# Gathering, turning and scoring all cached K during the projections of a hybrid decoder step

## The reference

```
q, k, v, z, f = split(rms_norm(x) @ w_in_attn)
logf = log_sigmoid(f + b_f);  c = cumsum(logf)
s = q.k / 8 + c[query] - c[key]          causal
y = (softmax(s) @ v * silu(z)) @ w_out
```

## Time and profile before

| | us |
|---|---|
| median of 3 runs (range) | 2210.48 (2210.18 to 2215.91) |
| the profiled execution's own time | 2207.72 |
| span of its trace | 2206.0 |
| projections, 797 to 1200 | 403 |
| seam and batch 0, 1200 to 1321 | 121 |
| batches 1 to 7, 1321 to 2058 | 737 |
| tail, from 2058 | 148 |

### The profile page before, as it was taken

One profiled execution on the slowest core, in us unless ns is written; L12 is line 12 of the kernel. 1 busy time (PEld: TensorE's weight loads), 2 busy tenths in 40 slices (PEclk: granted clock), 3 DMA queues, 4 the chain that ended last, 5 costly groups with the idle time before them and its releaser, 6 DMA issues. The chain is left out here.

```text
span 2206.0 us, 36290 instructions
## 1 busy us (share of the span) xinstructions
PE 1884.8 (85%) x13168; PEld 1343.1 (61%) x13168; DVE 1126.3 (51%) x1846; ACT 538.1 (24%) x1203; POOL 610.2 (28%) x691
## 2 busy tenths in 40 slices
PE   4999999999999799999997568776777786778797
PEld 3877777787787677887886244443444443434475
DVE  4444444454464561112231676766676767676523
ACT  4211211121121332112111123232323232323421
POOL 0000000000000001001001676665666665666010
PEclk9999999999999999999998679898988898989899
DMA  4111111111111213223225779999999999999861
GB/s 139 39 45 48 36 49 48 40 50 43 40 41 48 97 58 102 93 76 97 93 76 138 268 221 342 348 342 330 336 362 329 352 325 330 339 344 337 294 220 59
DMA packets 184781, 384.64 MB, mean 174 GB/s; under 512 B 21009, under 2 KB 99250, under 8 KB 184366
## 3 DMA queue, kind: packets, MB, share of 16 engines
q1 hardware_dynamic: 126796, 196.59, 26.3%
q0 software_dynamic: 57376, 185.06, 25.0%
q10 hardware_dynamic: 466, 0.88, 0.1%
HBM read 353.94 MB, written 29.22 MB: 174 GB/s over the span
## 5 line engine op out<-in xcount | busy, mean ns | idle before, releaser
L332 POOL DMA_INDIRECT k_raw<-in_cache_k_dram,k_idx x512 | 496.3, 969 | 285.4 <-DVE kt L1525 140.9
L1525 DVE STREAM_TRANSPOSE kt<-k_raw 128x1024 f32<-128x1024 f32 x256 | 315.0, 1237 | 108.3 <-DMA k_raw<-in_cache_k_dram,k_idx 106.6
L876 DVE TENSOR_TENSOR w_lo<-w_raw,w_hi 128x1024 fp32r<-128x1024 f32 x96 | 109.0, 1135 | 332.9 <-ACT w_hi L516 330.3
L673 PE MATMUL ps_a<-h_hi,w_hi 128*128 128x512 f32 x656 | 263.6, 402 | 0.0
L675 PE MATMUL ps_a<-h_hi,w_lo 128*128 128x512 f32 x656 | 258.6, 394 | 0.0
L674 PE MATMUL ps_a<-h_lo,w_hi 128*128 128x512 f32 x656 | 258.6, 394 | 0.0
L1273 PE MATMUL b<-con,p_p 128*128 128x128 f32 x432 | 89.2, 322 | 134.8 <-DVE p_p L1539 91.4
L425 POOL DMA_DIRECT2D out_dram<-g_out x4 | 2.2, 543 | 628.7 <-ACT g_out L563 628.7
L1273 PEld LDWEIGHTS b<-con,p_p 128*128 128x128 f32 x432 | 52.3, 155 | 177.7 <-DVE p_p L1539 77.9
L1251 PE MATMUL b<-kt,q_bd 128*32 128x256 f32 x2048 | 139.8, 419 | 19.7 <-DVE q_n L1550 19.5
L673 PE MATMUL ps_b<-h_hi,w_hi 128*128 128x512 f32 x384 | 153.0, 398 | 0.0
(11 more groups left out here) (295 smaller groups left out, 3135.5 us busy)
## 6 DMA issues: line engine op xcount, KB each, us to landing
v_pg<-in_cache_v_dram SPq DMA_DIRECT2D x256, 512.0 KB, 6.4
w_raw<-in_w_in_pool_dram SPq DMA_DIRECT2D x32, 512.0 KB, 4.0
w_raw<-in_w_in_attn_dram SPq DMA_DIRECT2D x32, 512.0 KB, 4.3
w_raw<-in_w_out_pool_dram SPq DMA_DIRECT2D x16, 512.0 KB, 3.6
k_raw<-in_cache_k_dram,k_idx POOLq DMA_INDIRECT x512
d_sb<-decay POOLq DMA_DIRECT2D x32, 256.0 KB, 7.7
qa<-q_aug POOLq DMA_DIRECT2D x8, 528.0 KB
ka<-k_aug POOLq DMA_DIRECT2D x8, 528.0 KB
```

Of the source, the lines that this page charges most:

```text
L332: pool.indirect_dma_start(k_raw[:, k, i, :], None, cache_rows, bass.IndirectOffsetOnAxis(ap=row, axis=0)).then_inc(k_full[k], 16)
L673: nc.tensor.matmul(ps, ah, bh, start=j == 0, stop=False)
L876: V.tensor_tensor(w_lo[slot][:, 0:width], raw[:, 0:width], w_hi[slot][:, 0:width].bitcast(F32), ALU.subtract).then_inc(dve_lo, 1)
L1525: V.transpose(kt[s % 2][:, :, 64 * k:64 * k + 64].rearrange("p i (t c) -> p t i c", c=32), k_raw[:, k, :, :].rearrange("p t (i c) -> p t i ...
```

## The change

All K work leaves the attention block. Whole rows of 4 KB are gathered, 4 indirect DMAs of 128 rows for a unit, so that a unit is now 128 rows of each of the four pages of a group with all 16 heads; there are still 64 units. DVE turns them during the projections, and PE scores one unit after each half of a prompt tile, 32 matmuls of 128 columns. ACT copies the scores out and stores them to `s_scr`; the attention block reads them back beside the decay. For this, q of all samples is made first, from eight raw weight tiles `wq`, and `sample_tile` of n = 0 falls away. silu(z) is stored to `z_scr` and read back when attention begins. The stores of q, k and rows move from POOL to SP, and V's first pages and `w_o` are loaded earlier. In the diff below some stretches are summed up in words; they stand in parentheses or after the name of an engine.

```diff
-    C_KB: 8 index columns;  cache_rows = cache_k[0] as half rows
+    C_KB: 4 index columns;  cache_rows = cache_k[0].rearrange("n k h d -> (n k) (h d)")
+        def k_quad(pool, u):
+            for k in range(4):
+                if u:
+                    pool.wait_ge(dve_kt, 4 * (u - 1) + k + 1)
+                pool.indirect_dma_start(k_raw[:, k, :], None, cache_rows,
+                                        bass.IndirectOffsetOnAxis(ap=k_idx[:, u, k:k + 1], axis=0)).then_inc(k_full[k], 16)
...
 SP, projections
+                sp.wait_ge(...); w_tile(0, 0), then w_query(k) for the eight wq tiles, spill of x1, wf
+                for f in range(KT8):
+                    for n in range(4):
+                        (waits as before) w_tile(f, n)
+                        n == 0: store_k(f - 1)       n == 1: store_k_rows(f - 1)
+                        n == 2: store_v_rows(f - 1)  (with k_sample and z_scr[f - 1])
+                        n == 3: store_q(f)
+                sp.wait_ge(pe_qk, UNITS)
+                for p in range(VR):
+                    v_load(sp, 1, p).then_inc(v_full[p], 16)
 POOL, projections
+                pool.wait_ge(spill, 16)
+                pool.wait_ge(dve_xn, 18)
+                pool.wait_ge(pe_pre, 1)
+                pool.wait_ge(dve_ix, 1)
+                for u in range(UNITS):
+                    (u == 12, 32: gather of the cached logf)
+                    (u == 60: qk_pair(pool, 0), v_pair(pool, 0))
+                    k_quad(pool, u)
 ACT, projections
+                def unit_out(b, s):
+                    u = b * QUADS + s
+                    act.wait_ge(pe_qk, u + 1)
+                    past(act, st_s[s % 2], b * (8 * QUADS) + 16 * (s // 2))
+                    nc.scalar.copy(ss_st[s % 2][:, :, :].rearrange("p h k -> p (h k)"), b5[:, 0:2 * PAGE]).then_inc(act_su, 1)
+                    act.wait_ge(act_su, u + 1)
+                    act.dma_start(s_scr[bass.ds(b, 1), :, :, PAGE * s:PAGE * s + PAGE].rearrange("o p h k -> p (o h) k"),
+                                  ss_st[s % 2][:, :, :]).then_inc(st_s[s % 2], 16)
 PE, projections
+                for half in range(2):            (made once: q of the samples)
+                    for k in range(KT8):
+                        mm = nc.tensor.matmul(ps_b[r:r + TS, c], h_s[:, k, :], wq[k][:, c], ...)
+                def unit_scores(b, s):
+                    past(pe, act_su, b * QUADS + s)
+                    pe.wait_ge(dve_kt, b * (4 * QUADS) + (4 * s + 4))
+                    for hh in range(2):
+                        for j in range(4):
+                            for cg in range(4):
+                                i = 16 * hh + 4 * cg + j
+                                mm = nc.tensor.matmul(b5[32 * cg:32 * cg + 32, PAGE * hh:PAGE * hh + PAGE], q_bd[:, i, :],
+                                                      kt[s % 2][:, i, :], start=j == 0, stop=j == 3, tile_position=(0, 32 * cg))
+                    mm.then_inc(pe_qk, 1)
+                proj:  n > 0: sample_tile
+                       half_tile(0), row_turn(j=0) for n >= 2, unit_scores(f, 2n)
+                       half_tile(1), add_parts for n > 0, row_turn(j=1) for n >= 2, unit_scores(f, 2n+1)
 DVE, projections
+                for n: lo; for j in 0, 1: rows_copy (n >= 2); k_turn(8f + 2n + j + 2); unit_queries(f + 1) at n = 3, j = 0
+                def k_turn(u):
+                    if u >= 2:
+                        dve.wait_ge(pe_qk, u - 1)
+                    for k in range(4):
+                        dve.wait_ge(k_full[k], 16 * (u + 1))
+                        V.transpose(kt[u % 2][:, :, 32 * k:32 * k + 32], ...).then_inc(dve_kt, 1)
...
 attention
-    PE: sample_scores(b, s) in each slot;  DVE: k_turn x4 in each slot, 16 copies into q_bd for a batch
-    POOL: k_quads in each slot
+    POOL: z_t[0], z_t[1..7] once; score_half loads s_in beside d_sb
+    DVE: sample_scores(b, s // 2) at even s: 2 adds of 128x256 from SBUF and one reduce
-    SP: w_o after pe_new of the last batch
+    SP: w_o in batch NB, ahead of its last 24 V pages, into tiles that wait for nothing
```

More of the change, by code:

```diff
@@ new lines, in build @@
+        pt_all = place("pt_all", [P, NB * PAGES], I32, big_at(AT_U + UW))
+        AT_K = 34584
+        k_raw = place("k_raw", [P, 4, DM], F32, big_at(AT_K))
+        kt = [place(f"kt{i}", [P, 32, PAGE], F32, big_at(AT_K + 4096 * (i + 1))) for i in range(2)]
+        wf = w_raw[1][:, :].rearrange("p (k n) -> p k n", n=P)
+        wq_at = [big_at(33792 + 1024 * k) for k in range(4)] + [big_at(AT_Y + 2048), at_in + 1280, big_at(19456), big_at(21504)]
+        wq = [place(f"wq{k}", [P, DM], F32, wq_at[k]) for k in range(KT8)]
@@ L257, in build @@
[L257 to L265, removed]
+        VR = 8
+        SW = PAST // 4 + TS
@@ L270, in build @@
[L270 to L277, removed]
+        wo_at = [big_at(n) for n in (9024, 10048, 0, 1024, 4160, 5184, 6208, 7232)]
@@ L593, in proj @@
                 def proj(f, first, last):
                     for n in range(4):
-                        ahead = first and n == 0
-                        if not ahead:
-                            px(f * 4 + (C_L0 + 2 + n + CR_W))
-                        if not ahead and not (last and n == 3):
+                        if n:
+                            px(f * 3 + smp_at(0, n))
+                        if not (first and n == 0) and not (last and n == 3):
                             act.wait_ge(ld_w[(n + 1) % 2], f * 32 + 16 * (33 + (n + 1) // 2))
@@ new lines, in proj @@
+                        unit_scores(f, 2 * n)
+                        half_tile(1, ps, slot, h_hi, h_lo, KT8).then_inc(tile_done, 1)
+                        if n:
+                            pe.wait_ge(act_px, f * 3 + (1 + PX_L0 + 1 + n))
+                            pe.wait_ge(act_b7, b7_at)
+                            add_parts()
+                        if n >= 2:
+                            row_turn(f, n, 1, more)
+                        unit_scores(f, 2 * n + 1)
+                        if n >= 2:
+                            pe.wait_ge(act_b7, b7_at + 1)
+                            nc.tensor.transpose(b7[0:TS, 0:P], (ks_st, vs_st)[n - 2][:, :], ident).then_inc(pe_b7, 1)
@@ L819, in _ @@
+                proj(0, extra(0))
+                forget_rows()
+                with pe.Fori(1, 3) as f:
+                    proj(f, extra(1))
+                page_totals(0, 2)
+                with pe.Fori(3, 6) as f:
+                    proj(f, extra(3))
+                page_totals(1, 5)
+                with pe.Fori(6, KT8) as f:
+                    proj(f, extra(6))
             @block.vector
@@ new lines, in page_decay @@
+                def page_decay(t):
+                    dve.wait_ge(pe_tri, t + 1)
+                    total = V.tensor_tensor(tot[:, t, :], tot[:, t, :], b4[:, 0:NH], ALU.add)
+                    total.then_inc(dve_tm, 1)
+                    dve.wait_ge(dve_tm, 1 + 12 * (t + 1) + 2 + t)
+                    for h in range(NH):
+                        last = V.tensor_scalar(pfx[:, h, :], pfx[:, h, :], -1.0, tot[:, t, h:h + 1], ALU.mult, ALU.add)
+                    last.then_inc(dve_dec, 1)
@@ L1599, in gate @@
                     r = P * QBLOCKS[s]
+                    first = isinstance(b, int) and b == 0
+                    dve.wait_ge(ld_z[0 if first else 1], 16)
                     z = z_t[:, bass.ds(b, 1), r:r + P].rearrange("p o t -> p (o t)")
@@ L1619, in sample_out, with batch @@
                     V.tensor_reduce(o_n[:, :], o_raw[:, :, :].rearrange("p h d -> p d h"), AX, ALU.add).then_inc(dve_ov, 1)
-                def batch(b, sample, more):
-                    if sample is False:
-                        for k in range(KR):
-                            k_turn(b, 0, k)
+                def batch(b, sample):
                     queries(b)
                     for s in range(SLOTS):
-                        ahead = (b, s + 1) if s < SLOTS - 1 else (b + 1, 0)
-                        ahead = ahead if more or s < SLOTS - 1 else None
                         prompt_max(b, s, 0)
```

637 lines of the change are left out of this document (352 added, 285 removed).

## The result

The change makes the kernel slower: 2249.7 us (median of 4 runs, 2238.4 to 2259.0) against 2213.2 us for the kernel before on the same chip; the ratio is 1.0159 with a 95% interval of 1.0106 to 1.0212. The forecast was 2160 us, faster. The profiled execution of the changed kernel took 2248.77 us with a span of 2247.0, 41 us more than the span before.

A forecast was written before the change was run, and what follows sets the result against it. PE was taken to bound the projections and DMA the attention. The terms 177 - 3 - 50 - 163 - 9 = -48 took the span from 2206 to 2158, forecast as 2160 us, with 2105 to 2230 for 8 in 10.

The forecast's parts named there:

- Projections: Projection stage: grows by 177 us, of which 163 for 64 units at 2.55 us and 12 for late K.
- Seam: Between projections and attention: 10 us becomes 7, since POOL no longer ends with stores; -3.
- Batch 0 with its stall: First attention batch and the wait before it: 112 us becomes 62, since nothing waits for K; -50.
- Batches 1 to 7: Later attention batches: 105.3 us each becomes 82, bounds 63 and 92; -163 over seven.
- Tail: After the batches: w_o loaded earlier ends ACT's wait for it; -9 (0 to -12).
- first rival: Projections: K's supply paces them, 10 us a unit, 2230 us in all, deciding from about 9.7; chance 0.17.
- late K: Projections: waits for K whose buffer slot returns late, 12 us (0 to 60).
- the 81 of the slots: Batches 1 to 7: 105.3 us less 19 from eight slots and 5 from the q/k wait.
- second rival: Batches 1 to 7 stay near 90 us as sample_scores filled PE's waits; 2218 us in all; chance 0.13.
- 10.5 us of other work: Batch start, kernel before: work covering part of ka's 16.3 us load, leaving about 8 us of PE idle.
- The slots' 62 us: Batch 0: 58 us from a line through two worked slots, 62 with new_scores, last values and a late q/k load.
- The upper bound (75): Batch 0: 75 us if the clock stays at the 0.76 seen before the change.

The follow-up runs named there:

- e11_supply: Changed kernel with a quarter of each unit's score matmuls in the projections, gathers and turns as they are: 2236.5 us.
- e4_nogather: Changed kernel with K's gathers left out in the projections, all but the first unit's: 2209.8 us.
- e13_nosupply: Changed kernel with a quarter of each unit's score matmuls and no gathers but the first unit's: 2137.6 us.
- e10_half: Changed kernel with 8 filler matmuls a slot in all batches and no other edit: 2210.4 us.
- c5_fill_half: Changed kernel with two q/k buffer pairs, lsel and half of w_o earlier, V pages behind stores, filler matmuls per slot (16 in batch 0, 8 later): 2163.9 us.
- e2_qk2: Changed kernel with two pairs of q/k buffers, batch b+1's heads loaded from slot 1 of batch b: 2217.4 us.
- e3_ends: Changed kernel with lsel loaded in the projections, first V pages behind the last stores, all of w_o loaded at the attention's start: 2227.4 us.
- e9_kraw2: Changed kernel with two buffers for gathered rows and one for turned ones, which also changed VectorE's order: 2296.1 us.

## Why the forecast was wrong

| Step | Forecast | Measured |
|---|---|---|
| Projections | +177 | +179 |
| Seam | -3 | +9.6 |
| Batch 0 with its stall | -50 | -30 |
| Batches 1 to 7 | -163 | -113 |
| Tail | -9 | -4.4 |
| Sum | -48 | +41 |

**Projections: the sum held, its terms did not.** That +177 met +179 is luck. A unit of 64 records takes 1.96 us on TensorE, not 2.55: splitting 256 columns into 128 cost next to nothing. With the few units that ran at the lower clock all 64 took 132 us, for 163. What filled the gap is waiting: VectorE's 120 us for `k_raw`, TensorE idle for 44 of the 576 us (6.5 of 403 before), and a clock of 0.96 for 1.00. The first rival's mechanism was thus at work. K's supply holds the stage at 575 us even with a quarter of the matmuls (e11_supply), 9.0 us a unit, under the 9.7 from which I let it decide; TensorE's own part is 546 (e4_nogather). Either alone covers most of the other, as e13_nosupply shows. The trace gives its length. On each of the four buffers, on the mean, 7.4 us pass from the start of a gather to the start of its turn (its landing, counted from the same start, has a median of 6.3), the turn takes 1.2, and 0.4 later the next gather starts: 9.0 us, in e11_supply too. The prediction had named this loop, "must come back within a unit's 8.9 us less its turn and issue, about 7 us", but had no row with a landing time and took 12 us for late K. That term was too small, as the 2.55 was too large.

Whether the loop's 6.3 us is a latency or the queues' load is only in part settled. For a latency: the four gathers of e4_nogather, with no other unit's behind them, landed in 5.4 to 7.0 us, median 6.1. Against it: DMA is busy 0.93 of the stage.

The rule of the Trainium skill weighed in the prediction (SBUF — State Buffer, "SBUF: two separate sides") does not show here either: GpSimd's gathers, beside a VectorE busy for 419 of 576 us, lasted as long as before in the median (937 for 946 ns); the mean rose from 969 to 1011 and the longest to 1.66 us. No row tells whether VectorE's turns run in a two-port mode, so the rule itself was not tested. The gathers' line, min/median/max in ns:

```profile
L347 POOL DMA_INDIRECT k_raw<-in_cache_k_dram,k_idx x249: 932/937/1655, 802.0 to 1364.0; - x125
```

**Batches 1 to 7: the step that failed.** "PE pauses more, and some stretches will stay at half clock. I take 82": 1 us was set aside for that, over the 81 of the slots. The slots' savings were read from matmuls of which most ran at the high level; once `sample_scores` was gone, the granted clock fell from 0.89 to 0.84. Give TensorE half of that work back as filler and a batch falls from 88.8 to 85.8 us (e10_half), or beside the second q/k pair from 85.4 to 81.4 (c5_fill_half), although the filler keeps TensorE busy for 9 us of it (56.6 over six batches): what the clock cost is these 3 to 4 us and whatever the filler itself takes. (Of e10_half's 3 us a batch, 1.3 are a shorter wait for `ka`.) This is the second rival, that `sample_scores` was what TensorE did while it waited; I gave it 0.13.

The other part is the q/k load. I had shortened it to 11 us "with K's 2 MB out of the queues"; it takes 15.1 us from issue to landing, nearly as before (16.3), since V's pages are what it shares the queues with. The one load with no V page under way, that for batch 1, shows it:

```profile
1471.13 8.03 DMA ka<-k_aug
```

The prediction's 10.5 us of other work behind the issue was misread too: 16.3 less 10.5 is not the 8 us of idle time that it names. Before, TensorE stood idle for 8.9 us at that place, so 7.4 were covered; in the changed kernel 15.1 less 7.7 is 7.4 again. TensorE's idle time stayed at 7.7 us a batch for the 3 forecast; e2_qk2 shows 4 us a batch for it. The two parts together are the 7 us that the forecast's 82 missed, and with both mended (c5_fill_half) the batch takes 81.4. That this is the forecast's figure is in part chance: the forecast kept 3 us of wait for q and k, and had no filler to run.

**Batch 0.** The slots' 62 us came from slots at full clock. It ran at 0.52, that is nearly all at 1.2 GHz, though TensorE was busy for 69 of 82 us: nothing but short transposes and scores with pauses between them. The upper bound (75) took the clock at 0.76, that of a batch with units in it; this bound was itself an effect of what the change removes. With filler it is 66 us (e10_half) to 75 (c5_fill_half). The step that failed is the same as in the batches: durations at the full clock were kept for a stretch that lost the work between its pauses.

**Seam.** I looked for POOL's stores, which did go, and did not follow SP's queue past the block's end: eight page loads in front of the last stores, then `lsel`. e3_ends shows that, taken together, all but 2.6 us of the 19 were this.

**Tail.** `w_o` waits for no semaphore any more, but SP's queue reaches it only at 2103.37, the end of the last batch: the V pages ahead of it are issued as TensorE frees their buffers. So ACT's first cast waited longer than in the earlier trace rows:

```profile
2113.75 1.04 ACT L1661 CAST wo_hi<-w_o 128x1024 fp32r<-128x1024 f32 x1 [7.78 <-DMA w_o<-in_w_out_attn_dram]
```

Loaded at the attention's start it leaves the chain (e3_ends). Seam and tail failed alike: a wait was taken away, and what stood ahead in SP's queue was not counted.

Left open: how much of the projections' +179 comes back with gathers a unit ahead, be it with room for both pairs of buffers (memory did not allow it) or with e9_kraw2's buffers and `lo` left where it was; and why 8 filler matmuls a slot do better than 16.

## What to carry to other kernels

Work on TensorE that fills its waits costs little there (8 added matmuls a slot made the changed kernel 39 us faster, 16 a slot 3 us slower). Moved to a stage where TensorE has no wait, it can be paid for twice: once in the new stage, which here grew by 179 us through the matmuls and the gathers side by side, and once in the clock of the old. Before a duration is taken from a trace for a kernel with less work, read the granted clock beside it and ask whether the work that goes was what kept it up; a few dummy matmuls test that in one run. Price a transfer that hands one buffer to and fro by its whole loop (issue, landing, use) beside engines and bytes. And when a buffer scheme is tried, keep the order of the other work on its engine, or the run shows the order and not the buffers.

## What the runs showed of the hardware

- Matmuls that nobody reads can make a kernel faster: 512 of them (128x256 f32, four column groups) took 39 us off 2249.7 and raised the granted clock of batches 1 to 6 from 0.84 to 0.94, that of batch 0 from 0.52 to 0.89.
- A TensorE 84% busy (69 of 82 us) was granted 0.52; one 92% busy (532 of 576) 0.96, and one 82% busy (474 of 575, e11_supply) 0.91. The busy share alone does not tell the clock, the less so as the same matmuls are busy for longer at the low one.
- A score unit of 32 matmuls of 128 columns in four column groups took 1.96 us at the median, 16 of 256 columns 1.93.
- A load of 528 KB for k, issued right behind one of 528 KB for q, landed in 8.0 us with no V page under way and in 14.6 to 15.4 us beside V pages.
- Four gathers of 128 rows of 4 KB with no others behind them landed in 5.4 to 7.0 us; beside a stage at 316 GB/s the median was 6.3.
- Eight issues of 512 KB from SyncE's queue took 8.4 us while the DMA engines were 0.86 busy.
